# In-place splitting of weight chunks from the gates on, and two expert slots filled in those stages, in a one-core decoder block

## The reference, cut to what matters

```
h = rms_norm(x, g_mix)
q, k, v (3 groups), retention q, k, v, g, gate_a, gate_r = split(h @ w_in)
A = dilated attention(q, k, v);  R = silu(g) * norm(retention(q, k, v))
merged = sigmoid(gate_a) * (A @ w_attn_branch) + sigmoid(gate_r) * (R @ w_ret_branch)
x = x + merged @ w_out
h2 = rms_norm(x, g_ffn)
x = x + hierarchical MoE(h2)      # 32 experts, top 1 group of 4, top 2 of its 8
out = rms_norm(x, g_final)
```

## Time and profile before

| what | value |
|---|---|
| median of 3 runs (lowest, highest) | 805.1 us (804.31, 805.18) |
| the profiled execution's own time | 804.96 us |
| its span, first to last instruction | 803.2 us |
| mean granted TensorE clock | 0.87 |
| PE busy, share of the span | 588.0 us, 73% |
| DVE busy | 249.7 us, 31% |
| ACT busy | 196.9 us, 25% |
| DMA | 255.82 MB, mean 318 GB/s |
| chain that ended last | PE 65%, DMA 30%, DVE 2% |

### The profile page before, as it was taken

The page is one execution under the profiler, slowest core; times in us unless marked ns, Lnnn a source line. Parts: engine busy times, 40 slices in busy tenths (PEclk is TensorE's granted clock), DMA queues, the critical chain, the costliest instruction groups (busy, mean ns, idle before and its releaser), DMA issues.

```text
span 803.2 us, 11626 instructions
## 1 busy us (share of the span) xinstructions
PE 588.0 (73%) x4469; PEld 419.7 (52%) x4469; DVE 249.7 (31%) x432; ACT 196.9 (25%) x290; POOL 13.5 (2%) x28
## 2 busy tenths in 40 slices
PE   3999999999999999965690780780770870960966
PEld 3999999999999998852320320320320320320321
DVE  6776675866664455571000010010010010010001
ACT  5454554565555443330000000000000000000001
POOL 3000000000000000010000000000000000000000
PEclk9999999999999999988795795795895795895887
DMA  8758658255686555899999999999999999999991
GB/s 235 236 141 261 174 166 261 78 158 157 167 241 194 185 182 187 338 401 408 428 427 426 428 428 426 425 431 423 428 428 426 431 426 423 432 429 423 431 397 54
DMA packets 92758, 255.82 MB, mean 318 GB/s; under 512 B 8640, under 2 KB 70080, under 8 KB 80448
## 3 DMA queue, kind: packets, MB, share of 16 engines
q1 hardware_dynamic: 90512, 255.35, 82.9%
q10 hardware_dynamic: 2224, 0.17, 0.2%
HBM read 254.45 MB, written 1.05 MB: 318 GB/s over the span
## 4 chain that ended last, share of the span: by engine, by line
PE 65%; DMA 30%; DVE 2%; ACT 1%; issue 1%; POOL 0%; SPq 0%; DVEq 0%; ACTq 0%
PE ps L1032 64%; DMA ring<-in_w_down 27%; DMA ring<-in_w_up 2%; DMA gain<-in_g_mix 1%; ACT work L581 1%; DVE hn L706 1%; DVE work L887 0%; PE ps L1111 0%; POOL rstd L488 0%; PE ps L1135 0%; DVE hn L1026 0%; ACT work L673 0%; DVE hT L714 0%; DVE split L682 0%; DVE work L890 0%
## 5 line engine op out<-in xcount | busy, mean ns | idle before, releaser
L1032 PE MATMUL ps<-store,work 128*32 128x512 f32 x128 | 73.6, 740 | 182.2 <-DMA ring<-in_w_down 182.2
L1032 PE MATMUL ps<-ring,work 128*32 128x512 f32 x896 | 186.4, 614 | 1.6 <-DVE work L964 0.9
L682 DVE TENSOR_TENSOR split<-ring,split 128x768 fp32r<-128x768 f32 (+2 forms) x132 | 120.8, 932 | 92.4 <-ACT split L533 91.8
L1032 PE MATMUL ps<-hT,split 128*128 128x256 f32 x1152 | 141.9, 286 | 1.8 <-DVE hT L714 1.8
L1032 PEld LDWEIGHTS ps<-hT,split 128*128 128x128 f32 x1152 | 140.3, 194 | 2.8 <-issue 2.3
L1032 PEld LDWEIGHTS ps<-store,work 128*32 128x32 f32 x128 | 16.1, 132 | 232.1 <-DMA ring<-in_w_down 168.7
L533 ACT ACTIVATE split<-ring 128x768 fp32r<-128x768 f32 (+2 forms) x132 | 107.3, 825 | 120.2 <-PE ps L1032 101.6
L1032 PE MATMUL ps<-split,hT 128*128 128x256 f32 (+2 forms) x672 | 106.5, 316 | 0.0
L1032 PEld LDWEIGHTS ps<-split,hT 128*128 128x128 f32 x672 | 98.1, 190 | 4.4 <-issue 0.5
L964 DVE COPY work<-ps 128x512 f32<-128x512 f32 x8 | 5.5, 692 | 254.6 <-PE ps L1032 254.6
L1032 PE MATMUL ps<-hT_slot,work 128*32 128x512 f32 x128 | 73.6, 740 | 0.0
(11 more groups left out here) (176 smaller groups left out, 474.8 us busy)
## 6 DMA issues: line engine op xcount, KB each, us to landing
ring<-in_w_up SPq DMA_DIRECT2D x24, 2048.0 KB, 34.7
ring<-in_w_gate SPq DMA_DIRECT2D x18, 2048.0 KB, 24.9
ring<-in_w_in SPq DMA_DIRECT2D x96, 192.0 KB, 3.9
oRT_slot<-in_w_down SPq DMA_DIRECT2D x8, 2048.0 KB, 26.2
mid<-in_w_up SPq DMA_DIRECT2D x8, 2048.0 KB, 34.3
store<-in_w_down SPq DMA_DIRECT2D x8, 2048.0 KB, 17.4
hT_slot<-in_w_down SPq DMA_DIRECT2D x8, 2048.0 KB, 21.8
ring<-in_w_in SPq DMA_DIRECT2D x96, 128.0 KB, 2.4
```

The lines of the kernel that those rows point to most:

```text
L682: dve.tensor_tensor(split[:, s, 1, 0:n], raw(s, n), split[:, s, 0, 0:n].bitcast(F32), ALU.subtract).then_inc(lo_ready, 1)
L1032: return pe.matmul(o, lhsT=l, rhs=r, start=start, stop=stop, skip_group_check=shared)
```

## The change

- From the gates on (`is_in_place`), the high part of chunk `s` goes to slot 1 and the low part is written over the raw chunk in slot 0. `split` is used up to the last retention quad. Slot 2 is free from the gates on.
- As the raw buffer is now read by PE (as the low part), SP loads the next quad's chunk after `chunk_used` instead of `lo_ready` (`after_use=True`), for all quads from `Q_GATE + 1` on.
- Up weight 3 of the first team (slot 2) is loaded in four quarters of 512 KiB, one per quad of gates. Down weight 1 (slot 9, `hT`) is loaded in four quarters, one behind each quad of `Q_WRET`, `Q_WRET + 1`, `Q_OUT`, `Q_OUT + 1`. They count on `early`.
- Down weight 2 (slot 6) is issued between `Q_OUT` and `Q_OUT + 1` of the chunk loads, where it came behind all of them and behind the load of the gain.
- Up 0 still waits for the last block of merged, but is now issued behind `Q_OUT + 1`'s loads. Up 1 and 2 wait for the projection's end, down 0 for the last read of x by DVE (`x2_ev`).
- merged is split into `merged_hi` (over `hn`) and `merged_lo` (in `work`) instead of `hT`.
- The four identity matmuls of x ahead of the projection are gone; DVE adds x in the eviction of the banks (a `tensor_tensor` in place of the copy). Four identity matmuls of `x2` behind the router's logits start the accumulation of the passes.

```diff
+        low_part = nc.alloc_sbuf_tensor_at("low_part", [P, CH, RAW], F32R, offset=ring_at)
+        high_part = nc.alloc_sbuf_tensor_at("high_part", [P, CH, RAW], F32R, offset=ring_at + 4096 * 4)
...
-            def load_quad(Q, piece):
+            def load_quad(Q, piece, after_use=False):
 
                 for s in range(CH):
-                    if not isinstance(Q, int) or Q > 0:
+                    if after_use:
+                        sp.wait_ge(chunk_used, CH * Q + s + 1 - CH)
+                    elif not isinstance(Q, int) or Q > 0:
 
                         sp.wait_ge(lo_ready, CH * Q + s + 1 - CH)
...
-            with sp.Fori(0, GI) as i:
-                load_quad(Q_GATE + i, columns_of(gates_v, 2, 256, i))
-            for Q, view, c in ((Q_ATTN, wattn_v, 0), (Q_WRET, wret_v, 0), (Q_WRET + 1, wret_v, CH),
-                               (Q_OUT, wout_v, 0), (Q_OUT + 1, wout_v, CH)):
-                load_quad(Q, full_rows(view, c))
+            load_quad(Q_GATE, columns_of(gates_v, 2, 256, 0))
+            sp.wait_ge(chunk_used, CH * Q_GATE)
+            quarter(U_AT[3], wu_v[3][:, bass.ds(0, 1024)], 0)
+            with sp.Fori(1, GI) as i:
+                load_quad(Q_GATE + i, columns_of(gates_v, 2, 256, i), after_use=True)
+                quarter(U_AT[3], wu_v[3][:, bass.ds(i * 1024, 1024)], i)
+            sp.sem_inc(up_loaded, 16)
+            load_quad(Q_ATTN, full_rows(wattn_v, 0), after_use=True)
+            for m, (Q, view, c) in enumerate(((Q_WRET, wret_v, 0), (Q_WRET + 1, wret_v, CH),
+                                              (Q_OUT, wout_v, 0), (Q_OUT + 1, wout_v, CH))):
+                load_quad(Q, full_rows(view, c), after_use=True)
+                quarter(D_AT[1], wd_v[1][:, bass.ds(m * 1024, 1024)], m)
+                if m == 2:
+                    sp.wait_ge(chunk_used, CH * (Q_WRET + 2))
+                    load_whole(0, wd_v, D_AT, (2,), down012_loaded)
+            sp.sem_inc(down012_loaded, 16)
...
-            sp.wait_ge(chunk_used, CH * (Q_WRET + 2))
-            load_whole(0, wd_v, D_AT, (2,), down012_loaded)
             sp.wait_ge(b_ready, KT // 2)
             load_whole(0, wu_v, U_AT, (0,), up_loaded)
-            sp.wait_ge(lo_ready, CH * QUADS)
-            load_whole(0, wu_v, U_AT, (1,), up_loaded)
             sp.wait_ge(chunk_used, CH * QUADS)
-            load_whole(0, wu_v, U_AT, (2, 3), up_loaded)
-            load_whole(0, wd_v, D_AT, (0, 1), down012_loaded)
+            load_whole(0, wu_v, U_AT, (1, 2), up_loaded)
+            sp.wait_ge(x2_ev, 2 * TT)
+            load_whole(0, wd_v, D_AT, (0,), down012_loaded)
...
-                act.activation(split[:, s, 0, 0:n], raw(s, n), ACT.Copy).then_inc(hi_ready, 1)
+                high_of = high_part[:, s, 0:n] if is_in_place(Q) else split[:, s, 0, 0:n]
+                act.activation(high_of, raw(s, n), ACT.Copy).then_inc(hi_ready, 1)
...
+                if is_in_place(Q):
+                    dve.tensor_tensor(low_part[:, s, 0:n], raw(s, n), high_part[:, s, 0:n].bitcast(F32),
+                                      ALU.subtract).then_inc(lo_ready, 1)
...
-                    dve.tensor_copy(x2[:, t, h * HALF:(h + 1) * HALF], bank(4 + 2 * t + h)).then_inc(x2_ev, 1)
+                    cols = slice(h * HALF, (h + 1) * HALF)
+                    dve.tensor_tensor(x2[:, t, cols], bank(4 + 2 * t + h), xs[:, t, cols], ALU.add).then_inc(x2_ev, 1)
...
             pe.wait_ge(bA_ev, KT // 2)
-            for t in range(TT):
-                for h in range(2):
-                    mm(ps[:, 4 + 2 * t + h, :], ident[:, :], xs[:, t, h * HALF:(h + 1) * HALF], True, False, True)
...
             ins.then_inc(logits_done, 1)
+
+            for t in range(TT):
+                for h in range(2):
+                    mm(ps[:, 4 + 2 * t + h, :], ident[:, :], x2[:, t, h * HALF:(h + 1) * HALF], True, False, True)
...
-                    pe.wait_ge(early, 16 * TEAM * PAIRS)
+                    pe.wait_ge(early, 16 * (TEAM * PAIRS + GI + 4))
```

More of the change, by code:

```diff
@@ L319, in raw, with parts, is_in_place @@
             return ring[:, 0, s * RAW:s * RAW + n]
-        def parts(s, n, steps):
-            return [split[:, s, a, 0:n].rearrange("p (k n) -> p k n", k=steps) for a in range(2)]
+        def parts(s, n, steps, in_place=False):
+            both = (high_part[:, s, 0:n], low_part[:, s, 0:n]) if in_place else (split[:, s, 0, 0:n], split[:, s, 1, 0:n])
+            return [one.rearrange("p (k n) -> p k n", k=steps) for one in both]
+        def is_in_place(Q):
+            return isinstance(Q, int) and Q >= Q_GATE
         slots = [ring[:, s, :] for s in range(6)] + [oRT_slot[:, :], mid[:, :], store[:, :], hT_slot[:, :],
@@ L419, in load_whole @@
                     sp.dma_start(slots[at[j]], expert(view, p, j)).then_inc(loaded, 16)
+            load_quad(Q_GATE, columns_of(gates_v, 2, 256, 0))
[14 more added lines that the diff above has]
+            sp.sem_inc(down012_loaded, 16)
+            sp.wait_ge(hn_done, TT)
+            sp.dma_start(gain[:, :], g_ffn.partition_broadcast(P)).then_inc(s_gain, 16)
             def load_last_down(p, n):
@@ L632, in _ @@
                 act.wait_ge(b_sum, b + 1)
-                act.activation(hT[:, 0, 2 * b:2 * b + 2, :], merged[:, 2 * b:2 * b + 2, :], ACT.Copy).then_inc(b_hi, 1)
+                act.activation(merged_hi[:, 2 * b:2 * b + 2, :], merged[:, 2 * b:2 * b + 2, :], ACT.Copy).then_inc(b_hi, 1)
             for s in range(CH):
@@ L875, in _ @@
                 dve.wait_ge(b_hi, b + 1)
[L876 removed]
+                dve.tensor_tensor(merged_lo[:, tiles, :], merged[:, tiles, :], merged_hi[:, tiles, :].bitcast(F32),
                                   ALU.subtract).then_inc(b_ready, 1)
@@ L1048, in transpose_rows, with quad @@
                             ins.then_inc(hT_psum, 1)
-            def quad(Q, n, steps, use, chunks=range(CH)):
+            def quad(Q, n, steps, use, chunks=range(CH), in_place=False):
                 for s in chunks:
                     pe.wait_ge(lo_ready, CH * Q + s + 1)
-                    ins = use(s, parts(s, n, steps))
+                    ins = use(s, parts(s, n, steps, in_place))
                     ins.then_inc(chunk_used, 1)
@@ L1164, in _ @@
                     pe.wait_ge(g_ready, 4 * i - 2 + 2 * m)
-                    quad(Q_GATE + m + 2 * i, W_G, 2, columns(4, 2 * m, W_G))
+                    quad(Q_GATE + m + 2 * i, W_G, 2, columns(4, 2 * m, W_G), in_place=True)
             def branch(outs_from, c0, tile_of, oT, n_c, done):
@@ L1181, in _ @@
             pe.wait_ge(roT_lo, RET_HEADS + 2)
-            quad(Q_ATTN, W_B, 1, branch(4, 0, lambda c: c, oAT, PAIRS, bA_done))
+            quad(Q_ATTN, W_B, 1, branch(4, 0, lambda c: c, oAT, PAIRS, bA_done), in_place=True)
             pe.wait_ge(g_ready, 2 * GI)
@@ L1199, in use @@
                         for h in range(2):
-                            ins = mm3(ps[:, 4 + 2 * t + h, :], [hT[:, a, j, t * P:(t + 1) * P] for a in range(2)],
-                                      [w[a][:, 0, h * HALF:(h + 1) * HALF] for a in range(2)], False)
+                            tokens = slice(t * P, (t + 1) * P)
+                            ins = mm3(ps[:, 4 + 2 * t + h, :], [merged_hi[:, j, tokens], merged_lo[:, j, tokens]],
+                                      [w[a][:, 0, h * HALF:(h + 1) * HALF] for a in range(2)], j == 0)
                             if j == KT - 1 and 2 * t + h < 3:
@@ L1205, in project_out @@
                 return use
-            quad(Q_OUT, W_B, 1, project_out(0))
-            quad(Q_OUT + 1, W_B, 1, project_out(CH))
+            quad(Q_OUT, W_B, 1, project_out(0), in_place=True)
+            quad(Q_OUT + 1, W_B, 1, project_out(CH), in_place=True)
             for t in range(TT):
```

17 lines of the change are left out of this document (10 added, 7 removed).

## The result

The changed kernel takes 807.53 us in the median of 7 runs (806.94 to 810.35), the kernel before 804.31 us (803.85 to 805.18). The ratio is 1.0049, 95% interval 1.0037 to 1.0061: slower by about 3.9 us, where +4.4 us was forecast. The profiled execution took 808.66 us, 3.70 more than the profiled one of before.

A forecast was written before the change was run, and what follows sets the result against it. PE bounds the kernel up to the first refill, transfers in the passes; 3.8 (load) + 2.1 (clock) - 1.5 (gather) = +4.4 us, forecast 809.4 us, range 806.0 to 813.5.

The forecast's parts named there:

- What bounds the kernel and what starts the stream: PE bounds up to the first refill and starts the stream at 362.25; then transfers bound; earlier backlog some 1.2 us.
- Early loads: Before the first refill: 4 MiB loaded early bring between nothing and 1.2 us; taken as nothing.
- Loads behind PE in the gates and branches: Gates and branches: loads waiting for PE's use stay covered by 1.1 to 1.9 us; taken as 0, ends 0 and +1.
- Rival A: Gates and branches: late chunks make PE wait in every quad, +3.5 us, 812.9 us; chance 0.19.
- The exposed load: Seam before the projection: PE waits for Q_OUT's chunk 3 to land and be split, +3.8 us, ends +3.4 and +4.9.
- The rule that HBM latency rises at high load: Landing of Q_OUT's chunk 3: up to 1.8 us longer by this rule, the sum up to 811.2.
- The clock at the projection: After 7 us idle the projection begins at 1.2 GHz for 4.2 us: +2.1 us, ends +1.5 and +2.9.
- The identity matmuls behind the logits: In PE's wait for the router: cost 0, keep the clock up so the gather gains, -1.5 us, ends -1.5 and 0.
- The tail: Last down matmuls, after idle time with 5.7 us of slow clock: 0 to -1.4 us; taken as 0.
- B: Projection, gather and tail: the clock holds, so about no change, +0.9 us, 805.9 us; chance 0.10.
- C: Before the first refill: bytes already bind the stream, so the change is faster, 799.6 us; chance 0.07.
- D: Quarters issued late behind SP's waits, so the pass waits for `early`; given no chance of its own.

The follow-up runs named there:

- late_loads: The changed kernel with up 3 and down 1 of the first team loaded whole at the projection's end, no quarters: 813.9 us, ratio 1.0124.
- before_wait: The kernel before, with only Q_OUT's chunks loaded after PE's use of the chunk a quad ahead instead of DVE's split: 809.81 us, ratio 1.0064.
- before_fill: The kernel before plus four identity matmuls of x2 behind the router's logits: 804.26 us, ratio 0.9999.
- alt_raw: The changed kernel with raw chunks in slot 9 from Q_WRET on, loads waiting for DVE's split only, down 1 loaded whole: 803.03 us, ratio 0.9997.
- reorder: The changed kernel with merged block 0's high part made ahead of high(Q_OUT, 3), and DVE's merge moved earlier to match: 806.55 us, ratio 1.0035.
- ident_back: The changed kernel with x added by PE's identity matmuls ahead of the projection again, none behind the logits: 809.29 us, ratio 1.0052.
- after_again: The changed kernel run anew, unchanged, beside the kernel before: 810.52 us, ratio 1.0075.
- fill_seam: The changed kernel plus eight identity matmuls of x in PE's wait ahead of the projection: 807.31 us, ratio 1.0046.
- alt_raw_split: As alt_raw, with one of the four identity matmuls of x2 moved ahead of the logits: 804.16 us, ratio 1.0005.

## Why the prediction was right

**What bounds the kernel and what starts the stream: right.** The first refill came 6.45 us later (1.25 of it the chance at the start) and the stream moved with it. Of this shift 0.66 came back at the seam, 0.97 in the stream and 1.1 in the tail, and 3.70 was left. In the ten other profiles, late_loads apart, down 3 lands 25.45 to 25.76 us behind the refill, 24.6 of it transfer by the prediction's count. That holds without early loads too, in before_wait and before_fill (25.53 and 25.46), where the refill came 1.5 and 1.7 us later behind the first eviction: the backlog of before was no more than that.

**Early loads, taken as 0 with -1.2 at most: -0.7 us** in this pair of profiles. The seam of 26.26 us shrank to 25.60, and the engines stood idle ahead of the refill, as forecast. What I did not see is that the price 0 holds against the kernel before only: the in-place parts move up 1 behind PE's last chunk, and without the early loads that would cost 4.4 us (late_loads). I counted this rightly in the prediction (6 MiB behind the projection) and wrongly in the expectation of that run.

**Loads behind PE in the gates and branches, taken as 0: right.** 576 records in 69.13 us without a gap. ACT's first `high` behind the sigmoids had to wait 0.15 us for its load, and DVE still finished 1.8 us ahead of PE, which by an estimate (2.88 us a chunk from 247.84 on) took up that chunk at 259.36:

```profile
255.21 1.06 ACT L555 ACTIVATE high_part<-ring 128x1024 fp32r<-128x1024 f32 x1 [0.15 <-DMA ring<-in_w_in]
256.30 1.23 DVE L705 TENSOR_TENSOR low_part<-ring,high_part 128x1024 fp32r<-128x1024 f32 x1 [0.52 <-ACT high_part L555]
```

The tightest places are elsewhere. By the same estimate `low` of the first chunk of the last gates quad ended 1.3 us ahead of PE (269.55 to 270.88), and that of the first chunk of `Q_WRET + 1` 1.0 us (304.40 to 305.44), where the prediction had 1.1 to 1.9. Rival A, stalls in every quad, is out, by that little.

**The exposed load, +3.8: measured +3.93**, by the chain that was worked out: landing 3.60 us (I took 3.2), then 1.06, 1.23 and 0.61. before_wait, which delays the four chunks of `Q_OUT`, shows it alone (+3.4), alt_raw takes it away. By reorder, the late load of chunk 3 and DVE's way behind the other late loads carry it together. The rule that HBM latency rises at high load (the Trainium skill, DMA: Bandwidth & Descriptors, Latency and other measured facts) would have allowed 1.8 us more. The landing was 3.07 us in late_loads with only down 2 behind it, 3.60 and 3.48 in the two profiles of the changed kernel and 3.19 in ident_back, with the quarter too: 0.5 us more at most, and not the same each time.

**The clock at the projection, +2.1: +1.32** in the profiled execution, +2.2 in that of after_again. The term is right and its size varies from execution to execution: 21.38 and 22.25 us to the first eviction against 20.06. fill_seam takes it away. The prediction's 4.2 us at half speed, called the middle of 3.0, 3.2 and 5.7, is neither their median (3.2) nor their mean (4.0). Measured were 2.8 and 4.7 us.

**The identity matmuls behind the logits, -1.5 at a cost of 0: this step failed.** "they keep PE busy where the clock now falls" was not what happened. The gather did gain 1.44 us, but the clock fell beneath the identity matmuls (0.59 in the stretch from 354), they took 5.38 us instead of 3.60, and the router's matmuls waited for them: +1.39. Net nothing in this execution, and a loss of 1.6 in after_again's (16.09 - 13.06 - 1.44). From the first eviction to the first refill it was 23.32 us before. Where the clock held up to the gather's end it was 21.9, the 1.4 to 1.5 us of the forecast (fill_seam, reorder, alt_raw). It was 24.9 to 25.0 in late_loads, before_fill and after_again, where the clock was low for longer, from the logits on. Alone, the matmuls gave nothing in the mean (before_fill, 0.9999). So what failed is "at a cost of 0": matmuls put in to keep the clock up can run at 1.2 GHz themselves and hold up what is behind them.

**DVE adds x, taken as 0: right.** The four evictions take 2.75 us in the chain against 2.73.

**The sum.** Forecast 3.8 + 2.1 - 1.5 = 4.4 at the first refill. Measured 3.93 + 1.32 - 0.05 = 5.2 there, and 4.5 at the landing of down 3, without the chance at the start. That the total came out so near is partly luck: the failed gain of 1.5 was made up by a cheaper clock and the seam. The tail, taken as 0 with -1.4 at most, gave 1.1 back, and this and the stream's 0.97 more than cancel the 1.25 of the start: 3.70. The two measurements, +3.9 and +6.0 us, lie on either side of the forecast.

**Rivals B and C.** B, the clock holding, is what fill_seam makes by force, and even then the kernel is at 1.0046, since the exposed load stays. Its profiled execution, the fastest of its five, took 806.00 us, near B's 805.9, though not by B's terms: the gather gained, the tail (12.47 us against 12.65) hardly did. C, bytes bind ahead of the refill, is wrong for the changed kernel and right for late_loads. As for D, no wait for `early` stands in the chain: pass 0's first gate matmul, at 364.71, is released by DVE after 0.87 us of idle time, as before.

## What to carry to other kernels

Writing a result over its input saves a buffer, but it moves every load behind it from "after the split" to "after the use". In a steady stage the other chunks covered that. Where an engine's program order puts a dependent step behind the late chunks, here the merge behind the `high` and `low` of `Q_OUT`, it did not, and a buffer of its own for these quads took the loss away (slot 9 in alt_raw, at the price of loading down 1 late). Loading early pays only if bytes bind at the end of the stretch that it empties. So count the bytes issued there, with those that the edit itself pushes into it, against its length.

## What the runs showed of the hardware

- The same wait of 3.16 us of PE was followed by a granted clock of 0.50 in one execution (alt_raw_split) and of 1.00 in another (alt_raw). In before_wait and ident_back waits of 3.10 and 3.26 us were followed by 0.50.
- The clock fell while PE had no gap: at about 346.5 us in before_fill, during float32 matmuls of 36 columns that had begun at 343.38 behind 0.85 us of idle time, and in the changed kernel at about 354.2 (to 357.6) under 512-column identity matmuls that followed such ones without an idle stretch.
- In the profiled executions such falls cost 1.3 to 2.7 us at the projection and up to 3 us at the router. The one with neither and without the exposed load (alt_raw's, 801.81 us) is 3 us faster than the profiled one of before. That the spread of the other runs comes from these falls is likely and not shown, as each version was profiled once.
